# Attention in pairs of units: turnings, scores and values of two units in blocks, four buffers of weights

## The chip, the cores and the metric

One core of a Trainium2 chip runs the whole program. Its engines are TensorE (PE: matmuls and transposes into PSUM, which has eight banks of 512 columns), VectorE (DVE), ScalarE (ACT), GpSimd (POOL) and SyncE (SP, which issues DMAs). Each engine takes its instructions in the order in which they are written and waits on semaphores. The metric is the time of one execution in device microseconds; for the kernel before it is 1221.78 us, the median of three runs (1221.78 to 1221.98).

## The reference, cut to what matters

Three layers over 512 tokens of width 1024: a gated linear attention, a sparse attention with three branches, and a stick-breaking attention with a pooling branch. The change is in the second. Its selection takes all eight key blocks (`n_top = min(16, 8)`) and its window is as long as the sequence, so the selected branch and the window branch are both full causal attentions, each with keys and values of its own:

```python
s = jnp.where(smask, jnp.einsum('bghtd,bgtksd->bghtks', qb, k_sel), NEG)
ps = jax.nn.softmax(s.reshape(...), axis=-1).reshape(s.shape)
o_s = jnp.einsum('bghtks,bgtksd->bghtd', ps, v_sel)
...
s = jnp.where(wmask, jnp.einsum('bghtd,bgsd->bghts', qb, kwin), NEG)
o_w = jnp.einsum('bghts,bgsd->bghtd', jax.nn.softmax(s, axis=-1), vwin)
...
gates = jax.nn.sigmoid(gl + b_gate).reshape(B, S, NSA_HEADS, 3)
o = jnp.einsum('bshc,bshcd->bshd', gates, out).reshape(B, S, NSA_Q) * jax.nn.silu(z)
return o @ w_out
```

There are 16 heads of 64 channels in 4 groups; z is a projection of the layer's input by 1024 columns of the input weights.

## The kernel before, in words

Products of full width are done in three matmuls of reduced-precision parts: a weight block (`raw`) is rounded by ACT to `w_hi` and the rest formed as `w_lo` by POOL or DVE, and activations are kept as `act_hi` and `act_lo`. Weight blocks are numbered (`C_NZ` is 32: four blocks for z; `C_NOUT` is 36: four output blocks), and blocks of even and odd number share two buffers each.

The stage in question works on 64 units (`unit(u)`). A unit is a tile t of 128 queries (u // 16), two heads (the two halves of the partitions), one of eight head pairs i, and one of the two branches w. Units 2x and 2x+1 are the two branches of pair x. A unit has (t + 1) x 128 keys. It passes through:

- `scores` (PE, L1814): for t = 0 one plain product a half, for others three products of rounded parts, into banks 0, 1 or 2, 3.
- `unit_max` (DVE, L2446): adds the mask, writes the negated scores into `prob` (three buffers, u % 3) and their minimum into `wstat`.
- `exponentials` (ACT, L1158): in place, with the sum.
- `unit_weights` (DVE, L2455): reciprocal of the sum. `scale` (POOL, L709): multiplies the weights by it and by the gate.
- `turn_weights` (PE, L1825): transposes the weights of half 0 into bank 4 and half 1 into bank 5.
- `turned_low` (ACT, L1165) and `turned_high` (DVE, L2461): copy them out to `probT` (two buffers).
- `values` (PE, L1840): weights by values into bank 6, both branches added up there; `pair_out` (DVE, L2468) adds that to the output `oT`.

On PE step u issues scores(u+2), a z piece, turnings of u-1 and values of u-2. The last two z blocks, two halves each, are done in pieces of four matmuls (`z_steps`, L1863) in bank 7, six pieces a half, in 24 of the steps from 0 to 27. ACT issues in step u exponentials(u+1), turned_low(u-1) and, in some steps, a copy of z or a rounding of something needed later: keys (`keys_high`), queries of the next tile (`queries_high`), weight blocks (`split_high`, `quarter_high`). DVE issues unit_max(u+1), pair_out, unit_weights(u), turned_high(u-1) and the low parts to those roundings. Everything here is a list written out at build time; only semaphores set the times. After the stage come the modulation rows (`mod_row`, L1876) and the output product (`out_and_turn`, L1409 first).

## Time and profile before

| | |
|---|---|
| median of the runs | 1221.78 us |
| the profiled execution | 1221.94 us |
| its span | 1220.2 us |
| PE, weight loads, DVE, ACT, POOL busy | 1204.6, 1019.5, 628.7, 560.9, 415.2 us |
| this stage, from 414.13 to 577.32 us | 163.19 us |

The page gives busy time, the chain of work that ended last, and groups of instructions. A matmul's duration includes the time in which the next is already running, so what PE spends on a piece is read from start to start in the timeline, not from durations. A weight load (PEld) is a row of its own.

### The profile page before, as it was taken

To read this page: it belongs to the slowest core of one execution; us is meant where nothing else is said; L and a number is where in the kernel's file an instruction comes from. 1 tells how busy PE (TensorE), PEld (TensorE's weight loads), DVE (VectorE), ACT (ScalarE), POOL (GpSimd) and SP (SyncE) were. 2 spreads that over 40 slices of the span, in tenths; PEclk is the share of its full clock that TensorE was granted. 3 is DMA by queue.
4 is the path that set the end of the run, shared out by engine and by line. 5 is a ranking of instruction groups with operands and counts; after the bars stand their busy time and mean duration, and the time that the engine had idled before them with its cause. 6 is when DMAs were issued, how large, how long until landed. Compare 5 with 4: busy or idle time off the path is not lost.

```text
span 1220.2 us, 19338 instructions
## 1 busy us (share of the span) xinstructions
PE 1204.6 (99%) x7763; PEld 1019.5 (84%) x7763; DVE 628.7 (52%) x1111; ACT 560.9 (46%) x1085; POOL 415.2 (34%) x295
## 2 busy tenths in 40 slices
PE   8999999999999999999999999999999999999998
PEld 7799879999887666678999887888888888888898
DVE  4587644876766466776380445444332760104434
ACT  5434245626522467767463435454544112443334
POOL 2434331110133354553305333222331644443441
PEclk9999999999999999999999999999999999999999
DMA  8325414577375130002122311222221333233321
GB/s 262 102 83 186 145 35 139 173 200 203 79 138 104 35 70 1 2 2 53 55 85 70 104 56 49 70 69 70 70 69 35 103 104 103 81 109 104 104 70 70
DMA packets 131265, 111.76 MB, mean 92 GB/s; under 512 B 38834, under 2 KB 128048, under 8 KB 131184
## 3 DMA queue, kind: packets, MB, share of 16 engines
q1 hardware_dynamic: 129696, 106.92, 30.1%
q10 hardware_dynamic: 1488, 3.71, 1.4%
q8 instruction: 57, 0.93, 0.3%
q14 instruction: 24, 0.20, 0.1%
HBM read 104.85 MB, written 2.10 MB: 88 GB/s over the span
## 4 chain that ended last, share of the span: by engine, by line
PE 93%; DVE 4%; ACT 2%; issue 1%; DMA 0%; POOL 0%; ACTq 0%; DVEq 0%
PE banks L1386 42%; PE banks L1375 13%; PE banks L1409 6%; PE banks L1476 3%; PE banks L1825 3%; PE banks L1840 3%; PE banks L1993 3%; PE banks L1814 3%; PE banks L1863 2%; PE banks L1943 2%; PE banks L2007 2%; PE banks L2038 1%; PE banks L1351 1%; PE banks L1546 1%; DVE w_lo L2093 1%; PE banks L1698 1%
## 5 line engine op out<-in xcount | busy, mean ns | idle before, releaser
L657 POOL TENSOR_TENSOR w_lo<-raw,w_hi 128x1024 fp32r<-128x1024 f32 x130 | 321.1, 2490 | 618.0 <-ACT w_hi L760 617.8
L1386 PE MATMUL banks<-act_hi,w_hi 128*128 128x512 f32 x704 | 277.4, 394 | 0.1
L1386 PE MATMUL banks<-act_lo,w_hi 128*128 128x512 f32 x704 | 274.4, 390 | 0.0
L1386 PE MATMUL banks<-act_hi,w_lo 128*128 128x512 f32 x704 | 274.3, 390 | 0.0
L760 ACT ACTIVATE w_hi<-raw 128x1024 fp32r<-128x1024 f32 (+1 forms) x160 | 158.9, 1043 | 124.9 <-PE banks L1386 97.5
L1386 PEld LDWEIGHTS banks<-act_hi,w_hi 128*128 128x128 f32 x704 | 132.3, 188 | 28.3 <-issue 1.3
L1386 PEld LDWEIGHTS banks<-act_lo,w_hi 128*128 128x128 f32 x704 | 132.1, 188 | 28.0
L1386 PEld LDWEIGHTS banks<-act_hi,w_lo 128*128 128x128 f32 x704 | 132.3, 188 | 26.5
L709 POOL TENSOR_SCALAR prob<-prob,wstat,gates 128x128 f32<-128x128 f32 (+3 forms) x128 | 79.5, 631 | 88.2 <-DVE wstat L2455 88.2
L1375 PE MATMUL banks<-w_hi,act_hi 128*128 128x256 f32 x384 | 109.2, 284 | 0.1
L1375 PE MATMUL banks<-w_hi,act_lo 128*128 128x256 f32 x384 | 108.7, 283 | 0.0
L1375 PE MATMUL banks<-w_lo,act_hi 128*128 128x256 f32 x384 | 108.7, 283 | 0.0
L1158 ACT ACTIVATE prob<-prob,wstat 128x128 f32<-128x128 f32 (+3 forms) x128 | 70.7, 554 | 45.1 <-DVE wstat L2446 44.9
L1375 PEld LDWEIGHTS banks<-w_hi,act_hi 128*128 128x128 f32 x384 | 73.7, 192 | 0.5 <-issue 0.4
L1375 PEld LDWEIGHTS banks<-w_lo,act_hi 128*128 128x128 f32 x384 | 73.7, 192 | 0.0
L1375 PEld LDWEIGHTS banks<-w_hi,act_lo 128*128 128x128 f32 x384 | 73.7, 192 | 0.0
L2446 DVE CUSTOM_DVE_ANT_0 prob<-banks,key_mask 128x128 f32<-128x128 f32 (+3 forms) x128 | 57.1, 483 | 3.4 <-PE banks L1814 3.4
L2461 DVE COPY probT<-banks 128x128 f32<-128x128 f32 (+3 forms) x64 | 31.4, 490 | 48.6 <-PE banks L1825 48.3
L1409 PE MATMUL banks<-w_hi,act_hi 128*128 128x256 f32 x192 | 54.9, 286 | 0.0
L1409 PE MATMUL banks<-w_hi,act_lo 128*128 128x256 f32 x192 | 54.3, 283 | 0.0
L1409 PE MATMUL banks<-w_lo,act_hi 128*128 128x256 f32 x192 | 54.3, 283 | 0.0
L2601 DVE TENSOR_TENSOR tmp<-banks,zh 128x512 f32<-128x512 f32 x8 | 5.5, 692 | 89.8 <-PE banks L2007 89.8
(431 smaller groups left out, 2419.3 us busy)
## 6 DMA issues: line engine op xcount, KB each, us to landing
raw<-w_in SPq DMA_DIRECT2D x32, 1024.0 KB, 5.7
raw<-gla_w_in SPq DMA_DIRECT2D x11, 1024.0 KB, 5.3
raw<-nsa_w_in SPq DMA_DIRECT2D x29, 256.0 KB, 4.5
raw<-nsa_w_in SPq DMA_DIRECT2D x6, 1024.0 KB, 6.5
raw<-gla_w_out SPq DMA_DIRECT2D x4, 1024.0 KB, 6.6
ada_first<-w_ada SPq DMA_DIRECT2D x4, 1024.0 KB, 8.0
raw<-nsa_w_out SPq DMA_DIRECT2D x16, 256.0 KB, 4.6
raw<-w_branch_a SPq DMA_DIRECT2D x4, 1024.0 KB, 5.1
```

Source lines behind the costliest of these rows:

```text
L657: pool.tensor_tensor(w_lo[:, u, k], raw[:, u, k], w_hi[:, u, k].bitcast(F32), ALU.subtract).then_inc(lo_done, 1)
L709: return pool.tensor_scalar(p, p, wstat[:, u % 4, 2, half:half + 1], gates[:, t, 3 * h + 1 + w:3 * h + 2 + w], ALU.mult, ALU.mult)
L760: act.activation(w_hi[:, u, k, 0:n], raw_of(c, u)[:, k, 0:n], ACT.Copy).then_inc(hi_done, 1)
L1158: act.activation(p, p, ACT.Exp, scale=-1.0, bias=wstat[:, u % 4, 0, half:half + 1], accum_out=wstat[:, u % 4, 1, half:half + 1]).then_inc( ...
L1375: mm = pe.matmul(b[:, t * CW:(t + 1) * CW], x[:, k, tok], w[:, u, k, :], start=(k == 0 and n == 0), stop=(k == KT - 1 and n == 2))
L1386: mm = pe.matmul(b[:], w[:, u, k, m * P:(m + 1) * P], x[:, k, :], start=(k == 0 and n == 0), stop=(k == KT - 1 and n == 2))
L1409: mm = pe.matmul(zone, x[:, k, tok], w[:, u, k, :], start=(start and n == 0), stop=(stop and n == 2), skip_group_check=True)
L1476: mm = pe.matmul(bank[2 * u + m][:, tok], w[:, u, k, m * P:(m + 1) * P], x[:, k, tok], start=(half == 0 and k == 0 and n == 0), stop=(k == ...
L1814: mm = pe.matmul(bank[2 * (u % 2) + half][:, 0:keys], q, k, start=(n == 0), stop=(t == 0 or n == 2))
L1825: mm = pe.transpose(bank[4 + half][:, k * P:(k + 1) * P], prob[:, u % 3, half, k * P:(k + 1) * P], ident[:])
L1840: mm = pe.matmul(bank[6][half * NDH:(half + 1) * NDH, 0:P], v_tok2[:, k, w, g * NDH:(g + 1) * NDH], probT[:, u % 2, half, k * P:(k + 1) * ...
L2446: last = dve.tensor_tensor_reduce(prob[:, u % 3, half, 0:keys], bank[2 * (u % 2) + half][:, 0:keys], key_mask[:, S - keys:S], -1.0, -NEG, ...
```

## The change

The stage is written over pairs x instead of units. PE issues in pair x the turnings of both its units, the scores of both units of pair x+2, one z piece of six matmuls (four pieces a half, 16 in all) and the values of both units. `prob` gets a fourth buffer, on memory of `pcT` for t below 2 and of `act_lo` from there on. For t below 2 both units' turned weights stand in one bank a half and are copied out by one instruction each on ACT and DVE; from t = 2 on the four turned pieces go to banks 4, 5, 7 and again 4, the last after ACT has copied the first. Roundings and low parts move: those of a weight block to pairs 4, 5 (`C_NZ + 3`) and 7, 8 (`C_NOUT`), of keys to pairs 1, 2, of queries to pairs 3, 11, 19, and of block `C_NOUT + 1`, in quarters, from units 28 to 34 to pairs 24 to 28. Of the modulation rows one half moves behind the last values. Names of variables in the diff: `NPAIR` is 32, `NUNIT` is 64.

```diff
 N_FIRST = 10
-Z_FROM, Z_STEPS, Z_SIZE = 0, 6, 4
+Z_STEPS, Z_SIZE = 4, 6
...
         assert probT.manual_sbuf_range[1] <= spare.manual_sbuf_range[1]
+        prob_small = over("prob_small", [P, 2, 2 * P], pcT)
...
-        LAST_SPLIT = Z_FROM + 4 * (Z_STEPS + 1)
-        split_next = {Z_FROM + (Z_STEPS + 1) * (q + 1): C_NZ + 3 + (q + 1) // 2 for q in (0, 1, 3)}
-
-        round_keys, round_queries = {1: 0, 4: 1}, {9: 1, 21: 2, 36: 3}
-
-        def z_piece_end(u):
-
-            q, r = divmod(u - Z_FROM, Z_STEPS + 1)
-            return q if r == Z_STEPS and 0 <= q < 4 else None
+        round_keys, round_queries = {1: 0, 2: 1}, {3: 1, 11: 2, 19: 3}
+        round_weights = {4: (C_NZ + 3, 0), 5: (C_NZ + 3, 1), 7: (C_NOUT, 0), 8: (C_NOUT, 1)}
+        LAST_SPLIT = 24
+
+        def z_piece_end(x):
+
+            return (x + 1) // Z_STEPS if (x + 1) % Z_STEPS == Z_STEPS - 1 and x + 1 < 4 * Z_STEPS else None
+
+        def prob_of(u, half, keys):
+
+            if u % 4 < 3:
+                return prob[:, u % 4, half, 0:keys]
+            return (prob_small if unit(u)[0] < 2 else prob_large)[:, half, 0:keys]
+
+        def turns_before(x):
+
+            return 2 * x if x < NPAIR // 2 else NPAIR + 4 * (x - NPAIR // 2)
+
+        def copies_before(x):
+
+            return x if x < NPAIR // 2 else NPAIR // 2 + 2 * (x - NPAIR // 2)
...
-            def turned_low(u):
-
-                keys = unit(u)[3]
-                act.wait_ge(t_full, 2 * u + 1)
-                act.activation(probT[:, u % 2, 0, 0:keys], bank[4][:, 0:keys], ACT.Copy).then_inc(t_low, 1)
+            def turned_low(x, w):
+
+                keys = unit(2 * x)[3]
+                act.wait_ge(t_full, turns_before(x) + 2 * w + 1)
+                if x < NPAIR // 2:
+                    act.activation(probT[:, :, 0, 0:keys], bank[4].rearrange("p (w n) -> p w n", w=2)[:, :, 0:keys], ACT.Copy)\
+                        .then_inc(t_low, 1)
+                else:
+                    act.activation(probT[:, w, 0, 0:keys], bank[(4, 7)[w]][:, 0:keys], ACT.Copy).then_inc(t_low, 1)
+
+            def part_high(c, part):
+
+                u = c % 2
+                if part == 0:
+                    more[u] += 48
+                    act.wait_ge(raw_landed[u], 16 * (c // 2) + 16 + more[u])
+                    act.wait_ge(bank_full[2 * u + 1], c // 2)
...
-            exponentials(0)
-            for u in range(NUNIT + 1):
-                if u + 1 < NUNIT:
-                    exponentials(u + 1)
-                if u:
-                    turned_low(u - 1)
-                q = z_piece_end(u)
+            for u in range(3):
+                exponentials(u)
+            for x in range(NPAIR):
+                turned_low(x, 0)
+                if 2 * x + 3 < NUNIT:
+                    exponentials(2 * x + 3)
+                if x == NPAIR - 2:
+                    act.preload_act_table_set("silu_and_others")
+                if x >= NPAIR // 2:
+                    turned_low(x, 1)
+                q = z_piece_end(x)
                 if q is not None:
                     take_z(C_NZ + 2 + q // 2, q % 2, bank[7])
-                if u == NUNIT - 1:
-                    act.preload_act_table_set("silu_and_others")
-                if u in round_keys:
-                    keys_high(round_keys[u])
-                elif u in round_queries:
-                    queries_high(round_queries[u])
-                elif u in split_next and u < LAST_SPLIT:
-                    c = split_next[u]
-                    split_high(c, c // 2, c % 2)
-                elif u >= LAST_SPLIT and u < LAST_SPLIT + 4:
-                    quarter_high(C_NOUT + 1, u - LAST_SPLIT)
+                if 2 * x + 4 < NUNIT:
+                    exponentials(2 * x + 4)
+                if x in round_keys:
+                    keys_high(round_keys[x])
+                elif x in round_queries:
+                    queries_high(round_queries[x])
+                elif x in round_weights:
+                    part_high(*round_weights[x])
+                elif LAST_SPLIT <= x < LAST_SPLIT + 4:
+                    quarter_high(C_NOUT + 1, x - LAST_SPLIT)
 
             for k in range(KT + 2):
...
-            def turn_weights(u):
-
-                t = unit(u)[0]
-                for half in range(2):
-                    pe.wait_ge(w_scaled, 2 * u + half + 1)
-                    if u:
-                        pe.wait_ge((t_low, t_high)[half], u)
+            def turn_pair(x):
+
+                t = x // 8
+                for n in range(4):
+                    w, half = (n % 2, n // 2) if t < 2 else (n // 2, n % 2)
+                    pe.wait_ge(w_scaled, 2 * (2 * x + w) + half + 1)
+                    if t < 2:
+                        zone = bank[4 + half][:, w * 2 * P:(w + 1) * 2 * P]
+                    else:
+                        zone = bank[(4, 5, 7, 4)[n]]
+                    if x == NPAIR // 2 and n == 2:
+                        pe.wait_ge(bank_free[2 * ((C_NZ + 3) % 2) + 1], (C_NZ + 3) // 2 + 1)
+                    if t >= 2 and n == 3:
+                        pe.wait_ge(t_low, copies_before(x) + 1)
+                    weights = prob_of(2 * x + w, half, (t + 1) * P)
                     for k in range(t + 1):
-                        mm = pe.transpose(bank[4 + half][:, k * P:(k + 1) * P], prob[:, u % 3, half, k * P:(k + 1) * P], ident[:])
-                    mm.then_inc(t_full, 1)
+                        mm = pe.transpose(zone[:, k * P:(k + 1) * P], weights[:, k * P:(k + 1) * P], ident[:])
+                    if t >= 2 or n % 2:
+                        mm.then_inc(t_full, 1)
...
                 t, i, w, keys = unit(u)
-                pe.wait_ge(t_low, u + 1)
-                pe.wait_ge(t_high, u + 1)
+                x = u // 2
+                if t >= 2 or w == 0:
+                    pe.wait_ge(t_low, copies_before(x) + w + 1)
+                    pe.wait_ge(t_high, copies_before(x) + w + 1)
                 if u == 0:
                     pe.wait_ge(c_taken, 4)
                 elif w == 0:
-                    pe.wait_ge(pv_read, u // 2)
+                    pe.wait_ge(pv_read, x)
                 for k in range(t + 1):
                     for half in range(2):
                         g = i // 4 * 2 + half
                         mm = pe.matmul(bank[6][half * NDH:(half + 1) * NDH, 0:P], v_tok2[:, k, w, g * NDH:(g + 1) * NDH],
-                                       probT[:, u % 2, half, k * P:(k + 1) * P],
+                                       probT[:, w, half, k * P:(k + 1) * P],
                                        start=(w == 0 and k == 0), stop=(w == 1 and k == t))
                 if w == 1:
...
-            def z_steps(u):
-
-                q, r = divmod(u - Z_FROM, Z_STEPS + 1)
-                if not (0 <= q < 4 and r < Z_STEPS):
+            def z_steps(j):
+
...
             scores(1)
-            for u in range(NUNIT + 2):
-                if u + 2 < NUNIT:
-                    scores(u + 2)
-                begins = u > Z_FROM and (u - Z_FROM) % (Z_STEPS + 1) == 0
-                if not begins:
-                    z_steps(u)
-                if u >= NUNIT - 1 and u < NUNIT + 1:
-                    mod_row(1, u - (NUNIT - 1))
-                if 1 <= u <= NUNIT:
-                    if u == 1:
-                        pe.wait_ge(c_read, 4)
-                    turn_weights(u - 1)
-                if begins:
-                    z_steps(u)
-                if u >= 2:
-                    values(u - 2)
+            z_steps(0)
+            scores(2)
+            scores(3)
+            pe.wait_ge(c_read, 4)
+            for x in range(NPAIR):
+                turn_pair(x)
+                for u in (2 * x + 4, 2 * x + 5):
+                    if u < NUNIT:
+                        scores(u)
+                z_steps(x + 1)
+                if x == NPAIR - 2:
+                    pe.wait_ge(s_max, NUNIT)
+                    mod_row(1, 1)
+                values(2 * x)
+                values(2 * x + 1)
+            mod_row(1, 0)
             pe.wait_ge(gain_ready, 1)
-            pe.wait_ge(t_low, NUNIT)
-            pe.wait_ge(t_high, NUNIT)
             pe.wait_ge(s_exp, 2 * NUNIT)
             mod_row(0, 0)
             mod_row(0, 1)
...
-            def turned_high(u):
-
-                keys = unit(u)[3]
-                dve.wait_ge(t_full, 2 * u + 2)
-                dve.tensor_copy(probT[:, u % 2, 1, 0:keys], bank[5][:, 0:keys]).then_inc(t_high, 1)
+            def turned_high(x, w):
+
+                keys = unit(2 * x)[3]
+                if x < NPAIR // 2:
+                    dve.wait_ge(t_full, turns_before(x) + 2)
+                    dve.tensor_copy(probT[:, :, 1, 0:keys], bank[5].rearrange("p (w n) -> p w n", w=2)[:, :, 0:keys])\
...
+            def last_low(quarter):
+
+                u, k = (C_NOUT + 1) % 2, slice(KT // 4 * quarter, KT // 4 * (quarter + 1))
+                if quarter % 2:
+                    dve.wait_ge(hi_done, 2 * (C_NOUT + 1) + quarter // 2 + 1)
+                else:
+                    dve.wait_ge(quarter_hi, 2 + quarter // 2)
...
-            for u in range(NUNIT + 2):
-                if u + 1 < NUNIT:
-                    unit_max(u + 1)
-                if u >= 4 and u % 2 == 0:
-                    pair_out(u // 2 - 2)
-                if u < NUNIT:
-                    unit_weights(u)
-                if 1 <= u <= NUNIT:
-                    turned_high(u - 1)
-                if u - 2 in round_keys:
-                    keys_low(round_keys[u - 2])
-                if u - 2 in round_queries:
-                    queries_low(round_queries[u - 2])
-                for part in range(2):
-                    if u - 1 - part in split_next and u - 1 - part < LAST_SPLIT:
-                        next_low(split_next[u - 1 - part], part)
-                    if u == LAST_SPLIT + 2 + 2 * part:
-                        dve.wait_ge(quarter_hi, 2 + part)
-                        next_low(C_NOUT + 1, part)
+            unit_max(1)
+            unit_weights(0)
+            unit_weights(1)
...
+            for x in range(NPAIR):
+                if 2 * x + 2 < NUNIT:
+                    unit_weights(2 * x + 2)
+                turned_high(x, 0)
+                if x:
+                    pair_out(x - 1)
+                if x >= NPAIR // 2:
+                    turned_high(x, 1)
+                if 2 * x + 3 < NUNIT:
+                    unit_weights(2 * x + 3)
+                for u in (2 * x + 4, 2 * x + 5):
+                    if u < NUNIT:
+                        unit_max(u)
+                if x - 1 in round_keys:
+                    keys_low(round_keys[x - 1])
+                elif x - 1 in round_queries:
+                    queries_low(round_queries[x - 1])
+                elif x - 1 in round_weights:
+                    next_low(*round_weights[x - 1])
+                elif LAST_SPLIT < x <= LAST_SPLIT + 4:
+                    last_low(x - 1 - LAST_SPLIT)
 
```

PE, 512 keys, the kernel before: two units. Names ending in `_low`, `score_k` and `score_q` are parts of keys and queries, a row with x2 is both halves.

```order
L1814 MATMUL banks<-score_k,score_q_odd 128x512 x2
L1814 MATMUL banks<-score_k,q_low_part 128x512 x2
L1814 MATMUL banks<-ks_low,score_q_odd 128x512 x2
L1825 MATMUL banks<-ident,prob 128x128 x8
L1840 MATMUL banks<-probT,v_tok_112 64x128 x8
L1814 MATMUL banks<-score_k,score_q_odd 128x512 x2
L1814 MATMUL banks<-score_k,q_low_part 128x512 x2
L1814 MATMUL banks<-kw_low,score_q_odd 128x512 x2
L1825 MATMUL banks<-ident,prob 128x128 x8
L1840 MATMUL banks<-probT,v_tok_112 64x128 x8
```

The same place in the changed kernel: one pair.

```order
L1864 MATMUL banks<-ident,prob 128x128 x8
L1864 MATMUL banks<-ident,prob_large 128x128 x8
L1845 MATMUL banks<-score_k,score_q_odd 128x512 x2
L1845 MATMUL banks<-score_k,q_low_part 128x512 x2
L1845 MATMUL banks<-ks_low,score_q_odd 128x512 x2
L1845 MATMUL banks<-score_k,score_q_odd 128x512 x2
L1845 MATMUL banks<-score_k,q_low_part 128x512 x2
L1845 MATMUL banks<-kw_low,score_q_odd 128x512 x2
L1882 MATMUL banks<-probT,v_tok_112 64x128 x16
```

The same matmuls stand in three blocks instead of six.

ACT, 128 keys, the kernel before, units 4 to 7: exponentials (L1158), copies of turned weights (L1165), the rounding of keys (L1184), a copy of z (L1128).

```order
L1184 ACTIVATE score_k<-kwT 128x1024
L1158 ACTIVATE prob,wstat<-prob,wstat 128x128 x2
L1165 ACTIVATE probT<-banks 128x128
L1158 ACTIVATE prob,wstat<-prob,wstat 128x128 x2
L1165 ACTIVATE probT<-banks 128x128
L1128 ACTIVATE silu_z_100<-banks 128x512
L1158 ACTIVATE prob,wstat<-prob,wstat 128x128 x2
L1165 ACTIVATE probT<-banks 128x128
L760 ACTIVATE w_hi<-raw 128x1024 x2
```

The changed kernel, ACT, pairs 2 to 4.

```order
L1180 ACTIVATE probT<-banks 128x2x128
L1172 ACTIVATE prob_small,wstat<-prob_small,wstat 128x128 x2
L1142 ACTIVATE silu_z_100<-banks 128x512
L1172 ACTIVATE prob,wstat<-prob,wstat 128x128 x2
L1212 ACTIVATE score_k<-kwT 128x1024
L1180 ACTIVATE probT<-banks 128x2x128
L1172 ACTIVATE prob,wstat<-prob,wstat 128x128 x4
L1219 ACTIVATE score_q_odd<-qT 128x512 x2
L1180 ACTIVATE probT<-banks 128x2x128
L1172 ACTIVATE prob_small,wstat<-prob_small,wstat 128x128 x2
L1172 ACTIVATE prob,wstat<-prob,wstat 128x128 x2
L1193 ACTIVATE w_hi<-raw 128x1024
```

One copy now stands for two, and there is a rounding in nearly every pair.

## Rows read from the trace of the kernel before

**Rows 1.** The page: busy time by engine, and the chain by engine.

```profile
PE 1204.6 (99%) x7763; PEld 1019.5 (84%) x7763; DVE 628.7 (52%) x1111; ACT 560.9 (46%) x1085; POOL 415.2 (34%) x295
PE 93%; DVE 4%; ACT 2%; issue 1%; DMA 0%; POOL 0%; ACTq 0%; DVEq 0%
```

**Rows 2.** Busy time by engine in the stretch of the stage.

```profile
core 0: us, PE busy (x) PEld busy (x) DVE busy (x) ACT busy (x) POOL busy (x), PEclk, DMA share, GB/s
414.13:577.32 163.19, 158.24 (x1439) 115.49 (x1437) 112.00 (x432) 113.63 (x344) 79.50 (x128) 1.00 0.10 24
```

**Rows 3.** Waits from 414 to 577 us: total us, times, longest.

```profile
PEld banks L1840 <- issue: 10.6, 59, 0.4
...
PEld banks L1825 <- POOL prob L709: 5.4, 7, 1.3
```

**Rows 4.** Timeline of PE, one unit at 512 keys: start, duration, instruction.

```profile
536.83 0.50 PE L1814 MATMUL banks<-score_k,score_q_odd 64*128 64x512 f32 x2
537.17 0.40 PE L1814 MATMUL banks<-score_k,q_low_part 64*128 64x512 f32 x2
537.41 0.39 PE L1814 MATMUL banks<-ks_low,score_q_odd 64*128 64x512 f32 x2
537.73 1.09 PE L1825 MATMUL banks<-ident,prob 128*128 128x128 f32 x8
538.75 1.09 PE L1840 MATMUL banks<-probT,v_tok 128*64 128x128 f32 x16
539.77 0.50 PE L1814 MATMUL banks<-score_k,score_q_odd 64*128 64x512 f32 x2
```

**Rows 5.** Timeline of PE, one unit at 128 keys with a z piece.

```profile
420.03 0.49 PE L1814 MATMUL banks<-first_k,qT 64*128 64x128 f32 x4
420.45 0.50 PE L1863 MATMUL banks<-act_hi,w_hi 128*128 128x512 f32 x1
...
421.25 0.40 PE L1863 MATMUL banks<-act_hi,w_hi 128*128 128x512 f32 x1
421.48 0.38 PE L1825 MATMUL banks<-ident,prob 128*128 128x128 f32 x2
421.79 0.44 PE L1840 MATMUL banks<-probT,v_tok 128*64 128x128 f32 x4
422.16 0.49 PE L1814 MATMUL banks<-first_k,qT 64*128 64x128 f32 x4
```

**Rows 6.** Timeline of PE at the stage's end: values of units 62 and 63.

```profile
573.54 2.04 PE L1840 MATMUL banks<-probT,v_tok 128*64 128x128 f32 x32
575.51 2.05 PE L1876 MATMUL banks<-ident,gain_mod 128*128 128x128 f32 x16
```

**Rows 7.** Timeline around the step to 384 keys: DVE's low parts, PE's waits.

```profile
483.18 1.40 DVE L2093 TENSOR_TENSOR w_lo<-raw,w_hi 128x1024 fp32r<-128x1024 f32 x1
...
487.29 0.63 PE L1825 MATMUL banks<-ident,prob 128*128 128x128 f32 x4 [0.91 <-ACT probT L1165]
...
488.29 1.33 DVE L2093 TENSOR_TENSOR w_lo<-raw,w_hi 128x1024 fp32r<-128x1024 f32 x1
...
492.44 0.84 PE L1825 MATMUL banks<-ident,prob 128*128 128x128 f32 x6 [1.01 <-ACT probT L1165]
```

**Rows 8.** Groups of ACT and DVE by shape, 409 to 578 us: busy, mean ns, idle before.

```profile
L1158 ACT ACTIVATE prob<-prob,wstat 128x512 f32<-128x512 f32 x32 | 22.9, 715 | 14.2 <-DVE wstat L2446 14.2
L1158 ACT ACTIVATE prob<-prob,wstat 128x384 f32<-128x384 f32 x32 | 19.4, 607 | 11.4 <-DVE wstat L2446 11.4
L1158 ACT ACTIVATE prob<-prob,wstat 128x128 f32<-128x128 f32 x32 | 12.5, 392 | 8.9 <-DVE wstat L2446 8.9
L1165 ACT ACTIVATE probT<-banks 128x384 f32<-128x384 f32 x16 | 7.5, 468 | 0.0
L1184 ACT ACTIVATE score_k<-ksT 128x1024 fp32r<-128x1024 f32 x1 | 1.1, 1055 | 0.0
...
L2446 DVE CUSTOM_DVE_ANT_0 prob<-banks,key_mask 128x384 f32<-128x384 f32 x32 | 16.4, 548 | 0.0
L2455 DVE RECIPROCAL wstat<-wstat 128x2 f32<-128x2 f32 x64 | 10.2, 159 | 1.0 <-ACT prob L1158 1.0
```

## What the change should do to the time

> **What bounds the kernel now.** I read the page first: TensorE (PE) is busy for 99% of the span and the chain that ended last is 93% PE [rows 1]. A busy PE is modelled, so this says only that PE is where to look. I then took the stretch that the change touches, from the second unit's scores at 414.13 us to the first product after the stage at 577.32 us: 163.19 us, PE busy 158.24, DVE 112.00, ACT 113.63, POOL 79.50, clock 1.00 [rows 2]. PE leads there too, and the other three have slack on the mean. The waits of the stretch split PE's loss in two [rows 3]: short ones put down to "issue", nearly one per unit (59 ahead of values, 0.18 us each), and a few long ones on POOL and ACT. The timeline shows what the first kind is.
>
> **The price of a block.** PE runs each unit as blocks: scores, turnings, values, and in 24 of the first units a z piece. At 512 keys a unit is 536.83 to 539.77, 2.94 us: scores 0.90, turnings 1.02, values 1.02 [rows 4]. With one key tile turnings take 0.31 and values 0.37 [rows 5]. Two points each give a slope and a rest: turnings 0.237 a key tile and 0.07 fixed; values 0.217 and 0.15 fixed. Scores step at 0.24 from group to group (537.17 to 537.41), three groups are 0.72, 0.18 is left [rows 4]. So each unit pays 0.40 us for its three changes of block, which the change halves. Without z a unit is 1.10 + 0.61 t us (t from 0 to 3).
>
> **The change part by part.** PE instructions stay the same in number and shape; they are regrouped.
> (1) Blocks of two units. 32 times a pair saves one set of fixed costs. Upper bound 32 x 0.40 = 12.8 us. The trace has one place where values of two units already stand together, 573.54 to 575.51: 1.97 us [rows 6], against 2 x 1.02, so only 0.07 was saved and not 0.15. (The second unit's copy may have been late there, so it is a lower bound.) With 0.07 for values the sum is 32 x 0.32 = 10.2. I take the middle, 0.11: 32 x 0.36 = 11.5 us.
> (2) z in 16 pieces of six instead of 24 of four. A piece of four takes 1.03 us (420.45 to 421.48) at a pitch of 0.23 to 0.24 [rows 5], so 0.1 is fixed: 8 x 0.1 = 0.8 us, bounds 0 and 0.9.
> (3) The low parts of the output weights' second block leave units 30 and 32, where they stood as two DVE pieces of 1.4 and 1.33 us ahead of the row minima of new scores. PE's turnings waited 0.91 and 1.01 us behind them [rows 7]: 1.9 us go. They are now four pieces in pairs 24 to 27, where one key row is 512 wide and a pair of PE is 2 x 2.94 - 0.36 = 5.5 us. ACT's round there (the sum of step 5, four exponentials of 0.72 [rows 8] and the rest scaled up by their ratio to 384 keys) is some 5.2, with a rounding quarter of about 0.6 it is 5.8 in four pairs: 0 to 1.2 us in all, taken at 0.1, since the mean durations used overlap in part. The load that waits for the last scores stands where it stood, about two pairs' turnings and values ahead of the stage's end, and has slack.
> (4) Two copies of turned weights become one of double width for t below 2. ACT and DVE issue 16 fewer each; ACT and DVE have slack [rows 2], so nothing is counted.
> (5) Added waits. Now an odd unit's exponentials stand behind the pair's copy on ACT, and DVE's reciprocal and the next minima stand behind them; behind ACT's waiting exponential stand the next copy and the rounding pieces, and PE's turnings wait for POOL's scaling of both units. Per pair ACT goes: exponentials of one unit, a gap (DVE reciprocal 0.16, two minima, handovers 0.25 by my estimate), exponentials of the next, copy. At 384 keys this is 1.21 + (0.16 + 1.10 + 0.25) + 1.21 + 0.47 = 4.4 us by the mean durations [rows 8], 4.2 if the handovers cost nothing, against PE's 2 x 2.33 - 0.36 = 4.3. Balanced: 8 pairs x 0 to 0.1, taken at 0.3 us. At one key tile, with 0.39 an exponential, the same sum is 2.7, and with a rounding piece of 1.05 it is 3.8 [rows 8], against PE's 4.26 (two units of 2.13, 420.03 to 422.16 [rows 5]) - 0.36 - 0.57 (two z matmuls and one entry fewer) = 3.3. Seven pairs carry such a piece where before they stood every few units: 7 x 0.5 = 3.5, of which about 1 is slack at the start. The kernel before pays 5.4 us for waits on POOL of this kind [rows 3], some 2 in this stretch: net +0.5. Pair 15 has no z piece, its 3.1 to 3.3 us of PE stand against a round near 4: +0.9. The z piece ahead of scores 2 and 3, and a first turning that needs both units: +0.3. With the 0.1 of (3) the sum added is 2.1 us, bounds 0.5 and 6.
> (6) The stage's end. DVE and ACT turn the attention output into the next product's operand from the last turned copy; one modulation row more now stands on PE behind the last values, so that work has more cover than before and nothing new is late.
>
> Sum: 11.5 + 0.8 + 1.9 - 2.1 = 12.1 us. The profiled execution took 1221.94 us (span 1220.2 and 1.7 around it): 1221.9 - 12.1 = 1209.8, and 0.16 less for the median of the runs, 1221.78: 1209.7 us. After the stage PE is the bound to the end and all moves up together. The rivals below are counted from 1221.8.
>
> **A rule that would change the sum.** z followed by turnings costs no entry: the last z matmul starts at 421.25 and the turnings at 421.48, a normal step of 0.23 [rows 5]. Scores are 64*128 tiles, values 128*64, z and turnings 128*128. If only a change of tile shape costs, the old order has three such changes a unit, 192; the new one puts z between scores and values, so a pair with z has four and a pair without has three: 15 x 4 + 17 x 3 = 111. At 0.40 / 3 = 0.133 each that is 81 x 0.133 = 10.8 us, with no z term of its own.
> The Trainium skill, "TensorEngine Tiling (Array Packing)", section Key Properties, states this as a rule: changing the tiling mode, as opposed to the tile, drains the engine. The step of 0.23 agrees with it, and it speaks against putting z where the change puts it.
>
> **The rivals.**
> A. Only shape changes cost, as just counted: 10.8 + 1.9 - 2.1 = 10.6 us, 1211.2 us. For it: the free z-to-turnings step. Against it: nothing; it shares most of its gain with the forecast.
> B. The round ACT-DVE-ACT becomes the bound. For it: 4.2 to 4.4 against 4.3 at 384 keys, 3.8 against 3.3 where pieces stand, and ACT idle on DVE today for 11.4 us over 16 such units [rows 8]. With 0.4 us more in the round: 8 x 0.4 at 384 keys, 7 x 0.4 at 128, nothing at 512: 6 us lost, 1215.7 us. Against it: the old order has such rounds and ran 2.94 a unit.
> C. Slower. The same round one whole us longer than I lay it out, because a late odd unit now stops both units' turnings. It decides once the round exceeds what two units took before: 4.66 at 384 keys and 5.88 at 512. Then the 384-key pairs cost 5.4 (+0.7 x 8), the 512-key pairs 6.1 (+0.2 x 8), the pairs with pieces 4.8 (+0.5 x 7), less some 6 gained at 256 keys and by (3): 4.7 us over, 1226.5 us. Against it: DVE and ACT are busy 69% of the stretch [rows 2].
> D. The change does not do what it says: PE's entries cost nothing by themselves and the issue waits fall to something else; only (3) and (5) remain, +0.2: 1222.0 us.
> E. More than forecast: 0.40 a pair in full and no added wait: 12.8 + 0.8 + 1.9 = 15.5 us, 1206.3 us.
>
> **How the numbers follow.** Forecast 0.50, own range 1207 to 1213; A 0.21; B 0.14; C 0.04; D 0.05; E 0.06. The two likeliest stand 1.5 us apart and share most of their terms, so the predicted time is 1209.7. For eight in ten: E's end is nearly reached, 1205.5; above, A is in and B's middle: 1216. Within 0.2% (2.4 us, about what a measurement of this kernel can tell from no change) fall D and the middle between B and C: 0.06. Faster 0.90, slower 0.04.
>
> **What would show it.** Right: pairs at 512 keys start 5.4 to 5.55 us apart (5.88 before), at 384 keys 4.2 to 4.4; the stage 150 to 152 us from its second scores to the first product, with the rest unchanged; issue waits on PE halved in count; the waits of 0.91 and 1.01 us gone; new PE waits on POOL around pairs 3 to 7 and 15 to 16. For A: values after z cost a full entry. For B: pairs at 384 keys near 4.8, each with a PE wait on POOL or ACT. Wrong: pairs at 512 keys above 5.7, or a gain that comes from outside the stage.

## The result and the profile after

The changed kernel took 1209.33 us (median of 4 runs, 1209.25 to 1209.45), the kernel before 1221.88 in the same session: a ratio of 0.9896, 95% interval 0.9879 to 0.9914. The forecast was 1209.7. The profiled execution has a span of 1207.5 us against 1220.2, 12.7 less. The page after, busy time and chain (answers to [rows 1]):

```profile
PE 1193.8 (99%) x7763; PEld 1019.6 (84%) x7763; DVE 626.8 (52%) x1097; ACT 558.7 (46%) x1069; POOL 411.8 (34%) x295
PE 93%; ACT 3%; DVE 3%; issue 0%; DMA 0%; POOL 0%; ACTq 0%; DVEq 0%
```

PE has as many instructions as before and is as full as before, and yet it is busy 10.8 us less: the busy time of a modelled PE counts the longer steps between its blocks too. The stage, from the same start, 414.13, to the same first product (answers to [rows 2]):

```profile
core 0: us, PE busy (x) PEld busy (x) DVE busy (x) ACT busy (x) POOL busy (x), PEclk, DMA share, GB/s
414.13:564.98 150.85, 147.31 (x1437) 115.43 (x1437) 114.01 (x420) 112.63 (x331) 76.54 (x128) 1.00 0.11 26
```

163.19 us became 150.85, at the same clock. The second unit's scores now start at 413.97, so from that mark the stage takes 151.01: 12.2 of the 12.7 us come from it, and 0.16 from ahead of it. Another 0.27 is in the output product that follows: its first turning had waited for DVE for 0.25 us before the change (618.12) and no longer does. Waits of the stage: total, times, longest (answers to [rows 3]):

```profile
PEld banks L1864 <- issue: 8.0, 37, 1.3
PEld banks L1882 <- issue: 6.3, 18, 0.4
PEld banks L1845 <- issue: 5.4, 27, 0.8
...
PEld banks L1882 <- ACT probT L1183: 5.0, 14, 0.9
...
PEld banks L1864 <- POOL prob L723: 2.7, 8, 1.1
...
PE banks L1864 <- ACT probT L1183: 1.9, 2, 1.0
PE banks L1882 <- ACT probT L1183: 0.7, 1, 0.7
```

L1845 is scores, L1864 turnings, L1882 values, L1905 z. Ahead of values the issue waits fell from 59 to 18. Another 14 are now named after ACT's copy; 13 of them are 0.25 us at 384 keys and 0.36 at 512, as are the issue waits beside them (0.25 at 480.51, 0.36 at 512.93), so they are the same entries under another name. The fourteenth is the 0.91. The timeline of PE, one pair at 512 keys (answers to [rows 4]):

```profile
535.88 1.09 PE L1864 MATMUL banks<-ident,prob 128*128 128x128 f32 x8
536.81 1.24 PE L1864 MATMUL banks<-ident,prob_large 128*128 128x128 f32 x8
537.98 0.51 PE L1845 MATMUL banks<-score_k,score_q_odd 64*128 64x512 f32 x2
...
539.57 1.97 PE L1882 MATMUL banks<-probT,v_tok 128*64 128x128 f32 x32
541.47 0.33 PE L1864 MATMUL banks<-ident,prob 128*128 128x128 f32 x1
```

A pair takes 5.59 us, two units took 5.88. Read start to start, turnings are 2.10 (two units: 2.04), scores 1.59 (1.80), values 1.90 (2.04). So scores and values gave back 0.35 together, and turnings, which also lost an entry, are longer than before. A pair at one key tile (answers to [rows 5]):

```profile
421.15 0.33 PE L1864 MATMUL banks<-ident,prob 128*128 128x128 f32 x1
...
421.74 0.72 PE L1845 MATMUL banks<-first_k,qT 64*128 64x128 f32 x8
422.38 0.50 PE L1905 MATMUL banks<-act_hi,w_hi 128*128 128x512 f32 x1
...
423.65 0.40 PE L1905 MATMUL banks<-act_lo,w_hi 128*128 128x512 f32 x1
423.98 0.66 PE L1882 MATMUL banks<-probT,v_tok 128*64 128x128 f32 x8
```

Here the last z matmul starts at 423.65 and values at 423.98, a step of 0.33 where two z matmuls stand 0.23 to 0.24 apart; the first z matmul takes such a step too (0.34, 422.38 to 422.72). Leaving z for turnings had cost nothing [rows 5]. Medians by kind of pair, start to start, in the kernel before (two units) and after:

| pair | before | after | of that z | saved without z |
|---|---|---|---|---|
| 128 keys, with z | 4.26 | 3.41 | 8 x 0.235, then 6 x 0.235 | 0.38 |
| 256 keys, with z | 5.40 | 4.53 | the same | 0.40 |
| 384 keys | 4.66 | 4.38 | none | 0.28 |
| 512 keys | 5.88 | 5.58 | none | 0.30 |

The kinds where a pair loses three changes of tile shape (384 and 512 keys) save less than those that lose two. The reason lies in the fourth turning. All engines, a pair at 384 keys (start, duration, instruction, in brackets the idle time before and its releaser):

```profile
495.70 0.87 PE L1864 MATMUL banks<-ident,prob 128*128 128x128 f32 x6
...
496.29 0.49 ACT L1183 ACTIVATE probT<-banks 128x384 f32<-128x384 f32 x1
496.31 0.36 PEld L1864 LDWEIGHTS banks<-ident,prob_large 128*128 128x128 f32 x3
496.41 1.03 PE L1864 MATMUL banks<-ident,prob_large 128*128 128x128 f32 x6
...
496.89 0.31 PEld L1864 LDWEIGHTS banks<-ident,prob_large 128*128 128x128 f32 x3 [0.23 <-issue]
```

The first turning (three of the first row's six matmuls, into bank 4) ends near 496.2, ACT copies bank 4 from 496.29 to 496.78, and only then can the fourth turning, whose zone is bank 4 again, begin. The second and third are done before that, and PE's weight load idles 0.23 us inside the block, labelled "issue".

At 512 keys there is a second part to this wait. In pairs 25 to 28 a quarter of a weight block is rounded just ahead of the copy. Pair 25:

```profile
525.02 0.61 ACT L1203 ACTIVATE w_hi<-raw 128x512 fp32r<-128x512 f32 x1
525.54 0.57 ACT L1183 ACTIVATE probT<-banks 128x512 f32<-128x512 f32 x1
```

The copy starts 0.81 us after the pair's first turning (524.73). In pair 24, without a rounding, it starts 0.72 after it. Turnings take 2.00 us in pairs 24 and 29 and 2.09 in pairs 25 to 28. So of the wait at 512 keys some 0.1 us is the bare chain and another 0.1 is ACT being late.

And the long waits that are left, in pairs 16, 20 and 30:

```profile
483.79 0.52 PE L1864 MATMUL banks<-ident,prob 128*128 128x128 f32 x3 [1.05 <-ACT probT L1183]
```

```profile
500.50 1.13 ACT L1219 ACTIVATE score_q_odd<-qT 128x512 fp32r<-128x512 f32 x2
...
502.15 0.52 PE L1864 MATMUL banks<-ident,prob 128*128 128x128 f32 x3 [0.87 <-ACT probT L1183]
```

```profile
555.25 1.28 ACT L1228 ACT_TABLE_LOAD   x1
...
557.19 1.09 PE L1882 MATMUL banks<-probT,v_tok 128*64 128x128 f32 x16 [0.67 <-ACT probT L1183]
```

In pair 16 (481.54) the copy stands behind ACT's late exponentials of the first unit at 384 keys; in pair 20 behind the rounding of queries, as it had before for 1.00 us; in pair 30 behind the load of ACT's table.

### The profile page after: what moved, and what is told of

It is laid out like the page before. It is cut to its first block, busy times and chain, and to the rows that moved or that the text cites. A ratio compares the mean times of both kernels' runs of the same rounds, so it can differ in the third digit from the quotient of the medians.

```text
span 1207.5 us, 19180 instructions
## 1 busy us (share of the span) xinstructions
PE 1193.8 (99%) x7763; PEld 1019.6 (84%) x7763; DVE 626.8 (52%) x1097; ACT 558.7 (46%) x1069; POOL 411.8 (34%) x295
## 4 chain that ended last, share of the span: by engine, by line
PE 93%; ACT 3%; DVE 3%; issue 0%; DMA 0%; POOL 0%; ACTq 0%; DVEq 0%
PE banks L1417 43%; PE banks L1406 13%; PE banks L1440 6%; PE banks L1507 3%; PE banks L1864 3%; PE banks L2028 3%; PE banks L1882 3%; PE banks L1845 3%; PE banks L1905 2%; PE banks L1978 2%; PE banks L2042 2%; PE banks L2073 1%; PE banks L1382 1%; PE banks L1577 1%; PE banks L1729 1%; PE banks L1678 1%
## 5 line engine op out<-in xcount | busy, mean ns | idle before, releaser
L774 ACT ACTIVATE w_hi<-raw 128x1024 fp32r<-128x1024 f32 (+1 forms) x156 | 154.9, 1043 | 124.8 <-PE banks L1417 97.4
L723 POOL TENSOR_SCALAR prob<-prob,wstat,gates 128x128 f32<-128x128 f32 (+3 forms) x96 | 57.4, 608 | 65.9 <-DVE wstat L2490 65.9
L1172 ACT ACTIVATE prob<-prob,wstat 128x128 f32<-128x128 f32 (+3 forms) x96 | 53.0, 553 | 28.0 <-DVE wstat L2481 28.0
L2481 DVE CUSTOM_DVE_ANT_0 prob<-banks,key_mask 128x128 f32<-128x128 f32 (+3 forms) x96 | 41.8, 484 | 4.4 <-PE banks L1845 3.6
L1882 PEld LDWEIGHTS banks<-probT,v_tok 128*64 128x64 f32 x640 | 34.3, 136 | 11.4 <-issue 6.3
```

The costliest lines, as they stand in the source:

```text
L723: return pool.tensor_scalar(p, p, wstat[:, u % 4, 2, half:half + 1], gates[:, t, 3 * h + 1 + w:3 * h + 2 + w], ALU.mult, ALU.mult)
L774: act.activation(w_hi[:, u, k, 0:n], raw_of(c, u)[:, k, 0:n], ACT.Copy).then_inc(hi_done, 1)
L1172: act.activation(p, p, ACT.Exp, scale=-1.0, bias=wstat[:, u % 4, 0, half:half + 1], accum_out=wstat[:, u % 4, 1, half:half + 1]).then_inc( ...
L1882: mm = pe.matmul(bank[6][half * NDH:(half + 1) * NDH, 0:P], v_tok2[:, k, w, g * NDH:(g + 1) * NDH], probT[:, w, half, k * P:(k + 1) * P], ...
L2481: last = dve.tensor_tensor_reduce(prob_of(u, half, keys), bank[2 * (u % 2) + half][:, 0:keys], key_mask[:, S - keys:S], -1.0, -NEG, ALU.ad ...
```

## The experiments

Diffs are against the changed kernel, except where it says otherwise. Times of PE's blocks are from start to start. The changed kernel was not run again beside the experiments. The kernel before was, at 1221.98 (experiments 1 to 4), 1221.73 (5 to 8) and 1221.81 us (9 to 11), where it had been 1221.88 beside the changed kernel, so differences from the changed kernel below are uncertain by some 0.15 us.

**1. The blocks taken apart again.** Same DVE, ACT and z; PE alone goes back to a unit at a time.

```diff
-                turn_pair(x)
-                for u in (2 * x + 4, 2 * x + 5):
-                    if u < NUNIT:
-                        scores(u)
+                for part in range(2):
+                    turn_pair(x, (2 * part, 2 * part + 1))
+                    if 2 * x + 4 + part < NUNIT:
+                        scores(2 * x + 4 + part)
```

> The changed kernel, with PE's turnings and scores of a pair taken apart again: turnings of unit 2x, scores of 2x+4, turnings of 2x+1, scores of 2x+5 (z and values stay as blocks of two; copies, buffers and the depth of two pairs stay). Theory 1 (the time is in PE's changes of block): 30 pairs pay one more entry of turnings (0.07) and of scores (0.18), 7.5 us, less some 2 us of waits that the looser turnings lose: about +5.5 us over the changed kernel, 1214.8, between 1213 and 1217. Rival (the gain came from the deeper pipeline and the fourth buffer, which hide latency): no change, 1209.3, or a little faster, since turnings wait less.

Measured: 1215.9 us (1215.52 to 1216.43), 6.6 above the changed kernel. One key tile:

```profile
421.02 0.44 PE L1864 MATMUL banks<-ident,prob 128*128 128x128 f32 x2
421.39 0.49 PE L1845 MATMUL banks<-first_k,qT 64*128 64x128 f32 x4
421.82 0.44 PE L1864 MATMUL banks<-ident,prob_small 128*128 128x128 f32 x2
422.18 0.49 PE L1845 MATMUL banks<-first_k,qT 64*128 64x128 f32 x4
```

Turnings and scores are 1.59 us in four blocks, 1.23 in two: two more changes of shape cost 0.36, so 0.18 each. At 384 keys the same edit costs only 0.12 a pair (4.50), at 512 keys 0.14 (5.72): between the turnings of the two units scores now stand, and the fourth turning finds bank 4 free. Its wait was therefore worth 0.24 and 0.22. Buffers, copies and the depth of two pairs were left as they are, so the rival, that these gave the gain, falls: 6.6 of the 12.5 us are the joined turnings and scores, and the wait takes part of it back. Values stayed joined here. What their blocks are worth rests on the timeline alone (1.90 against 2.04 us at 512 keys).

**2. z between turnings and scores.** No engine but PE is touched.

```diff
                 turn_pair(x)
+                z_steps(x + 1)
                 for u in (2 * x + 4, 2 * x + 5):
...
-                z_steps(x + 1)
```

> The changed kernel with the z piece between turnings and scores. Theory A (only a change of tile shape costs): turnings (128*128) to z (128*128) is free, so 15 pairs have three changes instead of four, each z block is shorter by 0.15 to 0.2 us and a pair at 256 keys starts 4.53 - 0.18 = 4.35 us after the one before; with 1.3 us of new waits, because scores come later, about 1207.9. Rival (each block costs its entry whatever stands before it): z blocks stay at 1.59 us, only the new waits are left: 1210.6.

Measured: 1207.44 us (1207.3 to 1208.14), ratio 0.9882 (0.9867 to 0.9898), 1.9 below the changed kernel. A pair at 256 keys:

```profile
454.16 1.09 PE L1864 MATMUL banks<-ident,prob 128*128 128x128 f32 x8
455.01 0.48 PE L1905 MATMUL banks<-act_hi,w_hi 128*128 128x512 f32 x1
...
456.25 0.40 PE L1905 MATMUL banks<-act_lo,w_hi 128*128 128x512 f32 x1
456.58 0.39 PE L1845 MATMUL banks<-score_k,score_q_odd 64*128 64x256 f32 x2
```

Turnings are 0.85 instead of 1.02, scores stay 0.90 and values 1.03: the pair is 4.35 instead of 4.53. From the 128\*128 tile of the turnings to that of z PE goes on at its step; the entry that is left is one. That is rival A's rule, at 0.175 us a change. At 128 keys about half of it is lost: in pairs 3 to 6 turnings wait for POOL's scaling and take 0.70 to 0.83 us, where those that don't wait take 0.41. Scores now stand a z piece later in the pair, which leaves less time from them to the scaled weights. That is a reading of the order, and no run tests it apart.

**3. The moved low parts alone, in the kernel before.** Diff against that kernel.

```diff
-        LAST_SPLIT = Z_FROM + 4 * (Z_STEPS + 1)
-        split_next = {Z_FROM + (Z_STEPS + 1) * (q + 1): C_NZ + 3 + (q + 1) // 2 for q in (0, 1, 3)}
+        LAST_SPLIT = 48
+        split_next = {Z_FROM + (Z_STEPS + 1) * (q + 1): C_NZ + 3 + (q + 1) // 2 for q in (0, 1)}
```

> The kernel before, with only the rounding and low parts of the second output weight block moved from units 28 to 32 to units 48 to 52. If those pieces caused the PE waits of 0.91 and 1.01 us at the step to 384 keys, these waits go; the two DVE pieces of 1.3 us now stand among 512-key units, where DVE has some 0.8 us of slack a unit, so about 0.6 us comes back at each: 1220.5 (1219.8 to 1221.2). If the waits belong to the step to 384 keys itself, 1221.9.

Measured: 1220.65 us (1220.53 to 1220.87), the kernel before 1221.98 beside it: 1.3 us, ratio 0.9989 (0.998 to 0.9998). The waits of 0.91 and 1.01 [rows 7] are gone from its timeline; the one of 1.00 behind the rounding of queries stands. Start to start the six steps around them, 14.34 us from 479.69 to 494.03 in the kernel before, are 11.88 here (479.80 to 491.68), 2.5 us less, more than the two waits together. The rest of the difference is what the moved pieces cost at their new place, two waits at 512 keys of 0.73 and 0.41 us, which lengthen their steps by 1.2 us:

```profile
536.17 1.06 PE L1825 MATMUL banks<-ident,prob 128*128 128x128 f32 x8 [0.73 <-ACT probT L1165]
```

So 1.3 us is a net figure, 2.5 less 1.2.

**4. Minima of the next even unit ahead of the odd unit's reciprocal.** DVE alone: it should let ACT's exponentials start sooner, and with them copies.

```diff
+                if 2 * x + 4 < NUNIT:
+                    unit_max(2 * x + 4)
                 if 2 * x + 3 < NUNIT:
                     unit_weights(2 * x + 3)
-                for u in (2 * x + 4, 2 * x + 5):
-                    if u < NUNIT:
-                        unit_max(u)
+                if 2 * x + 5 < NUNIT:
+                    unit_max(2 * x + 5)
```

> The changed kernel, with DVE's minima of unit 2x+4 ahead of the reciprocal of unit 2x+3. Theory (in the changed kernel the round exponentials, reciprocal, minima, exponentials sets how late ACT copies the first turned piece, and the fourth turning waits for that copy, 0.18 us a pair at 384 keys and 0.12 at 512): ACT's next exponentials start earlier, turnings at 384 keys shrink from 1.67 to about 1.5 us and the wait of 1.05 us at the first 384-key pair to some 0.3: 1207.5 (1206.8 to 1208.5). Rival (the longer turnings are the price of four pieces or of the buffer on the other memory): turnings stay at 1.67, 1209.3; or slower, if POOL's scaling, now later by the minima, comes too late.

Measured: 1209.74 us (1209.65 to 1209.91), 0.4 above the changed kernel. The theory falls on two counts. The fourth turning costs what it did: turnings in undisturbed pairs at 384 keys stay 1.67, so ACT was not late for that copy there; the copy follows the first turning at once and the chain turning, copy, turning is simply longer than two turnings. And what the wait in pair 16 gave back (1.05 became 0.33) a new one took:

```profile
431.12 2.71 POOL L723 TENSOR_SCALAR prob<-prob,wstat,gates 128x128 f32<-128x128 f32 x4 [1.10 <-DVE wstat L2490]
...
431.35 1.30 DVE L2533 TENSOR_TENSOR kw_low<-kwT,score_k 128x1024 fp32r<-128x1024 f32 x1
...
433.02 0.33 PE L1864 MATMUL banks<-ident,prob 128*128 128x128 f32 x1 [0.95 <-POOL prob L723]
```

POOL's scalings by line, 430 to 437 us of the same kernel (duration in ns, lowest, median, highest):

```profile
L723 POOL TENSOR_SCALAR prob<-prob,wstat,gates x7: 447/448/1414, 429.6 to 436.9; 128x128 f32<-128x128 f32 x7
```

A scaling of 447 ns took 1414 where it began (at 431.57) inside DVE's subtraction of 1.30 us. In the changed kernel DVE started that piece at 431.79, 0.44 us later, and the two scalings of that time took 0.88 together. The Trainium skill, "SBUF — State Buffer", section "SBUF: two separate sides", has a rule that fits: a DVE operation with two inputs in SBUF and a GpSimd operation that reads SBUF want the same ports, and whichever is second waits until the first is done. 431.35 + 1.30 is 432.65, and the turning that waited for the scaling ran at 433.02; the trace agrees, to 0.1 us. DVE is held up too where POOL came first, by little: a subtraction of this size takes 1.22 us where no scaling overlaps it (442.93 in the changed kernel), 1.30 where it begins 0.23 us before one ends (431.79) and 1.40 with 0.33 us (483.18 in the kernel before). The kernel before has the same collision:

```profile
L709 POOL TENSOR_SCALAR prob<-prob,wstat,gates x2: 447/928/1409, 427.4 to 427.9; 128x128 f32<-128x128 f32 x2
427.71 1.23 DVE L2493 TENSOR_TENSOR kw_low<-kwT,score_k 128x1024 fp32r<-128x1024 f32 x1
429.31 0.33 PE L1825 MATMUL banks<-ident,prob 128*128 128x128 f32 x1 [0.75 <-POOL prob L709]
```

Two more of its scalings are as long (1442 ns from 435.2, 1645 ns for 256 columns from 449.9). In the changed kernel no scaling of 128 or 256 columns takes more than 558 ns: its new places for these pieces happen to miss POOL.

**5. Three packed turnings at 384 keys.** Four pieces of three key tiles are twelve turned blocks, which fill three banks of four. The fourth piece is spread over the free quarters, so no bank is used twice.

```diff
+                if t == 2:
...
+                    last = prob_of(2 * x + 1, 1, (t + 1) * P)
+                    for n in range(3):
+                        zone = bank[(4, 5, 7)[n]]
...
+                        for k in range(t + 1):
+                            pe.transpose(zone[:, k * P:(k + 1) * P], weights[:, k * P:(k + 1) * P], ident[:])
+                        pe.transpose(zone[:, 3 * P:4 * P], last[:, n * P:(n + 1) * P], ident[:]).then_inc(t_full, 1)
```

> The changed kernel; at 384 keys the fourth turned piece goes in three blocks to the spare quarter of banks 4, 5 and 7, so that no bank is written twice in a pair; three copies of 512 columns take the place of four of 384. Theory (turnings at 384 keys are 0.14 us longer than their twelve steps because the fourth piece waits for a chain turning, ACT's copy, turning through bank 4, whatever else ACT does): turnings take 12 x 0.117 + 0.13 = 1.53 instead of 1.67 us in each of eight pairs, and the wait of 1.05 us in pair 16, also for that copy, shrinks: 1208.0 (1207.3 to 1208.6). Rival (the fourth buffer's place, or four pieces in a row, make the turnings long): 1.67 stays, 1209.3.

Measured: 1208.65 us (1208.52 to 1208.76), 0.7 below. The block itself gave more than I expected of it:

```profile
491.26 0.52 PE L1866 MATMUL banks<-ident,prob 128*128 128x128 f32 x3
491.61 0.27 PE L1867 MATMUL banks<-ident,prob 128*128 128x128 f32 x1
...
492.69 0.45 PE L1850 MATMUL banks<-score_k,score_q_even 64*128 64x384 f32 x2
```

Turnings take 1.43 us instead of 1.67 in each of the undisturbed pairs, 0.24 less, the same figure as in experiment 1, and the pair 4.20 instead of 4.38 (values are 0.06 longer). Eight times 0.18 would be 1.4. The rest was lost to waits: those of 1.05 in pair 16 and 0.87 in pair 20 became 0.93 on POOL and 0.44 on ACT, but pair 20 still takes 5.21 us (5.23 before), pair 21 waits another 0.34 for POOL, and pair 24 waits 0.37 for ACT's copy and takes 5.95 instead of 5.49. The copies of 512 columns take 0.60 us on ACT instead of 0.49, and a start now needs both units scaled; that these two made the new waits is not shown by a run.

**6. The last rounding of queries in pair 13 instead of 19.**

```diff
-        round_keys, round_queries = {1: 0, 2: 1}, {3: 1, 11: 2, 19: 3}
+        round_keys, round_queries = {1: 0, 2: 1}, {3: 1, 11: 2, 13: 3}
```

> The changed kernel with the rounding of the last query tile in pair 13 instead of pair 19. If the wait of 0.87 us in pair 20 is ACT's two roundings standing ahead of its copy, it goes, and pair 13, which has a z piece and so slack on ACT, shows none in its place: 1208.5. If the wait only moves: 1209.3.

Measured: 1208.57 us (1208.54 to 1208.82), 0.8 below. The wait of 0.87 is gone (turnings of pair 20 take 1.67), and none came at pair 13: there z gives ACT room.

**7. All five edits together:** z between, queries in pair 13, the table load behind the last copy it had delayed, minima first from pair 15 on, and the packed turnings.

```diff
-                if x == NPAIR - 2:
-                    act.preload_act_table_set("silu_and_others")
                 if x >= NPAIR // 2:
                     turned_low(x, 1)
+                if x == NPAIR - 2:
+                    act.preload_act_table_set("silu_and_others")
...
+                if 2 * x + 4 < NUNIT and x >= 15:
+                    unit_max(2 * x + 4)
```

> z between turnings and scores, the last query tile rounded in pair 13, the activation table loaded after the last but one copy on ACT, DVE's minima first from pair 15 on, and the packed banks at 384 keys. If the parts add up: 1207.4 - 0.85 - 0.67 - 0.7 - 1.1 = 1204.1 (1203.5 to 1205.5). If the waits only move from one place to the next, about 1206.5.

Measured: 1210.03 us (1209.95 to 1210.3), slower than the changed kernel, 6 us off what I expected. Of the five, z between, queries early and the packed turnings had each helped alone, minima first had not, and the table load had not been run alone. Pairs at 384 keys take 4.94 us. One of them:

```profile
489.51 0.16 DVE L2511 RECIPROCAL wstat<-wstat 128x2 f32<-128x2 f32 x1
...
489.77 1.30 POOL L727 TENSOR_SCALAR prob<-prob,wstat,gates 128x384 f32<-128x384 f32 x2 [2.17 <-DVE wstat L2511]
...
491.21 0.52 PE L1866 MATMUL banks<-ident,prob 128*128 128x128 f32 x3 [0.72 <-POOL prob L727]
```

POOL idles 2.17 us for DVE's reciprocal, then scales, and PE's first packed turning waits for the odd unit's weights. The reciprocal stands behind two minima of the next unit, and the packed block can't begin with the even unit alone. That closes a ring through all four engines, which is rival B in another kernel.

**8. The same without the packed turnings.**

> As e7_all, without the packed banks: 1205.2; the difference to e7_all is the price of the bank written twice, 1.1 us, or 0 by its rival.

Measured: 1205.71 us (1205.33 to 1206.01), ratio 0.9867 (0.9851 to 0.9884). So the edit that had brought 0.7 alone cost 4.3 here.

**9 to 11. Which of the two closes the ring.** Experiment 8 without minima first (9), experiment 7 without it (10), and 7 with it in pair 15 alone (11). The diff is 11 against 7.

```diff
-                if 2 * x + 4 < NUNIT and x >= 15:
+                if x == 15:
                     unit_max(2 * x + 4)
```

> The changed kernel with three edits: z ahead of scores (1.9 us less when alone), the last rounding of queries in pair 13 (0.8 less when alone), and the table load behind the last copy (0.67 less in the trace of e8). If the edits add, 1209.3 - 1.9 - 0.8 - 0.7 = 1205.9 us. The kernel with minima first from pair 15 as well took 1205.7; if minima first helps by itself at 384 and 512 keys, this one is 1 us or more slower, 1206.7; if it only moves a wait, 1205.9.

> As the run of all edits, 1210.0 us, without minima first. Theory: the packed turnings need both units scaled at their start, and minima first delays the reciprocal of the odd unit by the minima of the next even one, so the round ACT-DVE-ACT set the 384-key pairs at 4.94 us. Without minima first these pairs go back to 4.2 and the kernel takes 1204.9 to 1205.7 us. Rival: the packed order itself, with z ahead of scores and no slack from the long waits, makes the round the bound: pairs above 4.6 at 384 keys and 1208 us or more.

> As e10, with minima first in pair 15 alone, where it takes a wait of 1.05 us in the changed kernel down to 0.33. Theory: one pair of it shortens the first wait at 384 keys and delays nothing later: 1204.3 to 1205.2 us, 384-key pairs 4.2. Rival: the packed pair 16 needs both units at its start and loses what minima first gave: as e10 or 0.5 us slower.

Measured: not packed, three edits, 1205.67 us (1205.53 to 1205.89); packed, no minima first, 1204.92 (1204.76 to 1205.12), ratio 0.9861 (0.9845 to 0.9878); packed, minima first in pair 15, 1205.4 (1205.3 to 1205.46). Minima first is worth nothing without packing (1205.67 against 1205.71) and 5.1 us the wrong way with it. In pair 15 alone it also costs 0.5, as the rival of that expectation had it and not the theory: the first packed turning of 384 keys waits 1.34 us for POOL instead of 0.82. The same place in the packed kernel without it:

```profile
486.25 0.17 DVE L2511 RECIPROCAL wstat<-wstat 128x2 f32<-128x2 f32 x1 [0.41 <-ACT prob L1176]
...
487.98 0.17 DVE L2511 RECIPROCAL wstat<-wstat 128x2 f32<-128x2 f32 x1 [0.50 <-ACT prob L1176]
...
488.25 1.31 POOL L727 TENSOR_SCALAR prob<-prob,wstat,gates 128x384 f32<-128x384 f32 x2 [0.42 <-DVE wstat L2511]
```

Here the reciprocal waits for ACT, so it comes as soon as the exponentials are there, POOL is done at 489.56 and PE's next packed turning starts at 489.70 without a wait: pairs take 4.21. This kernel, 16.9 us below the one before and 4.4 below the changed one, is the best found.

## Why the prediction was right, point by point

The total was right to 0.4 us and the mechanism was right too. But that it came so near is partly luck: the blocks gave 1.4 to 1.8 us less than forecast, terms (3) and (5) together 1.5 to 1.9 more, and the two errors cancelled.

(1) and (2), the blocks and z, 11.5 + 0.8 = 12.3 forecast. Gross they are worth more. Experiments 1 and 2 price a change of tile shape at 0.18 and 0.17 us, say 0.175, and the rule section counted 81 of them: 14.2 us. The step that was mis-sized is the fixed part of turnings, 0.07. Its point at one key tile, 0.31, came from a unit that PE entered from z, and that entry is free. A unit without z of the kernel before (427.02 to 427.39) has 0.37: with that point the slope is 0.217 and the fixed part 0.15. Scores gave back 0.21 and values 0.15 in full (1.90 at 512 keys), not the 0.11 that I took between it and the bound from [rows 6]. Whether a late copy made that bound too low, as I suspected, is not shown. A set of three is 0.51 us, not 0.40.

Against it stands a term that the prediction did not have. For t from 2 on, the fourth turning uses bank 4 again. Front and diff show the wait; I priced ACT's and DVE's rounds and never the chain inside PE's own block. By experiments 1 and 5 it costs 0.24 us at 384 keys, by experiment 1 some 0.22 at 512 where a rounding quarter stands ahead of the copy: in 16 pairs at most 3.7 us. So 14.2 - 3.7 = 10.5, and the table of pairs above gives 8 x 0.38 + 8 x 0.40 + 8 x 0.28 + 8 x 0.30 = 10.9.

The 0.8 for z went wrong in its cause. Fewer, larger pieces save nothing as such: six matmuls take 1.59, of which 0.18 is fixed, four took 1.03 with 0.09, so per pair it is 0.18 either way.

(3) The waits of 0.91 and 1.01 are gone. I counted them as 1.9 us, but by experiment 3 the steps around them were 2.5 longer for the moved pieces, so the term was too small. That the pieces made waits of 1.2 us at 512 keys in experiment 3 doesn't count here: the changed kernel has them as quarters, and turnings of a pair with one take 0.09 more, 0.4 us in four pairs, where I had taken 0.1.

(5) Added waits, 2.1 forecast. What is left of the stage's 12.2 us after 10.5 to 10.9 is 1.3 to 1.7 for (3) and (5) together, where I had 1.9 - 2.1. With 2.5 for (3), the other waits are 0.8 to 1.2 us longer than before. The new ones exist: 1.05 in pair 16, 0.67 behind the table load, 0.36, 0.19 and 0.10 on POOL in pairs 4 to 6, and the very first turnings take 1.25 us where an undisturbed pair takes 0.59, 0.7 where I had 0.3. But long ones of the kernel before on POOL went too, as their total on PEld shows (5.4 us, now 2.7). One of them is the collision of experiment 4: its block of turnings took 0.8 to 0.9 us longer for it. No term of the prediction had that. By place I was near at pair 15 (0.9 forecast, 1.05 came, one pair later and on ACT's copy instead of POOL) and at t = 0 (0.5 forecast, 0.65 came). The 0.3 at 384 keys did not come: the round fits. (6) The table load ahead of a copy, 0.67 us, was my miss; I had written that nothing new is late at the end.

The rivals. A had the right rule with too low a price: at 0.133 it gave 10.8 us for (1), at 0.175 it gives 14.2. Of its signs, values behind z do cost an entry: z's first step is 0.34 and its last 0.33 instead of 0.235, together 0.2 us, where a piece of the kernel before, with turnings behind it, had the first alone. The Trainium skill's sentence in "TensorEngine Tiling (Array Packing)", section Key Properties, held against this kernel: the move of z that it speaks for brought 1.9 us. B did not happen here (4.38 at 384 keys, not 4.8), but experiment 7 shows what its ring looks like. C and D are excluded by the pairs; E's price of 0.40 was too low and its "no added wait" wrong.

Signs: 512-key pairs 5.49 to 5.59, most of them 5.57 to 5.59 and so a little over (5.4 to 5.55 forecast), 384-key pairs 4.38 (4.2 to 4.4), stage 150.85 (150 to 152).

Open: how the 0.8 to 1.2 us of the other waits divides. The waits before and after have different neighbours, and no experiment took them one at a time. The 2.5 of (3) is read in the kernel before, and no run puts the pieces back in the changed one. The fourth turning at 512 keys could not be taken out by itself, since sixteen turned blocks need four banks; 0.22 rests on experiment 1 and on a change costing there what it costs at one key tile, and its halves on pairs 24 and 25 alone, since no run took the rounding quarters away.

## What to carry to other kernels

Count changes of tile shape in the order of matmuls, not blocks, and price one in the trace by two places that differ in nothing else; a two-point fit is only good if both points were entered in the same way. When blocks are joined, look inside the new block for a buffer used twice: a chain matmul, copy, matmul that used to have other work in the middle now stands bare. An experiment that moves work instead of removing it measures a net: look in its trace for what the work costs at the new place. And an edit that helps alone may close a ring with another: packed turnings gave 0.7 us alone and cost 4.3 with minima first, which by itself gave nothing.

## What the runs showed of the hardware

- A change of tile shape, between 128\*128 tiles and 64\*128 or 128\*64 ones, costs PE 0.17 to 0.18 us of start-to-start time on the mean of those that experiments 1 and 2 added or took away; turnings to z and z to turnings, both 128\*128, cost none.
- The chain of turning into a bank, a copy of it by ACT and the next turning into that bank leaves PE 0.2 us idle at 384 keys, even when two turnings stand between (0.23 in the row at 496.89), and the profile calls it "issue".
- A scaling on POOL of 447 ns took 1414 ns when it began inside a subtraction of 1.30 us on DVE, and 1409 and 1442 ns at two such places of the kernel before. The subtraction takes 1.22 us alone and 1.30 to 1.40 where it begins 0.23 to 0.33 us before a scaling ends.
